# One decoder step on one core: the last gate's product on plain f32 operands, with the third tile's column halves side by side

## The chip, the cores and the metric

One core of a Trainium2 chip runs the whole step as one program. The metric is the device time in microseconds; lower is better. The engines are TensorE (PE, with its weight loads shown as PEld), VectorE (DVE), ScalarE (ACT), GpSimd (POOL) and SyncE (SP, which here only issues DMAs). They run their own instruction streams and meet at semaphores.

## The reference, cut to what matters

The step takes 256 prompt tokens and 64 sample tokens (8 sequences of 8), 320 rows of 1024 columns, through one layer. All that matters for the change is its last part:

```python
x1 = layer_norm(ALPHA * x + merged @ w_o, ln1_g, ln1_b)
x2 = layer_norm(ALPHA * x1 + hier_moe(x1), ln2_g, ln2_b)
gate = sigmoid(x2 @ w_ple_gate + b_ple_gate)      # (320, 1024) @ (1024, 1024)
pe = p_emb @ w_ple                                # (320, 256) @ (256, 1024)
x3 = layer_norm(ALPHA * x2 + gate * pe, ln3_g, ln3_b)
```

All inputs and outputs are f32.

## The kernel before, in words

The 320 rows lie in three tiles of 128, 128 and 64 rows (`TILES`, `ROWS`). Weights pass through `ring`, 12 slots of 128 x 2048 f32 (8 KB in each partition); SP fills a slot when the last reader of its former content has signalled. The program goes: input projection and attention, mixing and first norm, routing, 32 experts, and the tail. Everything up to the last expert is the same in both kernels.

**Precision.** PE takes two kinds of operands here. Plain f32 operands give one matmul that the trace shows as two records. Rounded operands (float32r, made by `rounded`) give one record. Before the change the gate's product is put together from rounded parts: an operand is cast to a high part, the low part is what the cast left out, and three products are summed (high x high, low x high, high x low). `by_parts` (L1387) writes this for the output projection w_o (L1625) and for the gate (L1856).

**The tail, in the order of its steps.**

1. The expert results lie transposed and sorted in `YsT`. `turn_sorted` (L1819) turns them back by PE, ten halves of 512 columns through banks 6 and 7; ACT casts each half to `yj_high` (L804), DVE subtracts to `yj_low` (L1311), and `combine` (L1828, matmuls at L1833) sums them into banks 0 to 5, one for each tile's column half. The first tile's combining is interleaved with the turns; the other two tiles follow in 40 matmuls. A turn may only begin when DVE's subtraction has freed its bank (`yt_v`).
2. Between these steps ACT and DVE prepare the gate's weights from the four ring slots of `w_ple_gate` (slots 1 to 4): ACT casts eight pieces of 128 x 1024 to `gw_high` (`high_gate`, L796 to L800) and DVE makes eight pieces of `gw_low` (`low_gate`, L1291 to L1295), each written into its engine's program at a fixed place.
3. DVE adds the residual (`combined`, L1285) and runs the second norm (`norm2`, L1305): statistics, their combination, one pass, a wait for ACT's square root (`norm`, L699), a reciprocal and a last pass. `layer_norm` (L1058) is the shared body.
4. `turn_tile` (L1376, transposes at L1384) turns a tile of x2 on PE, ACT casts the columns to `x2_high` (`high_columns`, L810) and DVE makes the low columns (`low_columns`, L1297).
5. PE runs six gate jobs (L1847 to L1857), two column halves of 512 for each tile, in turn into banks 7 and 6. For tiles 0 and 1 a job is 24 matmuls of 128 x 128 by 512 columns. For tile 2 the 64 high and 64 low rows lie side by side in one stationary operand of 128 columns (`x2_high` is 64 columns longer for this); a job is 8 such matmuls and 8 of the low weights, and its result stands in two halves of the bank's partitions, to be added. The turn of tile 1 stands before job 1, that of tile 2 before job 3. Job j waits for the bias add of job j - 2 (`pg_add`).
6. For each job DVE adds the bias (`gates`, L1329; for tile 2 a second add, L1337, brings in the other half of the partitions), ACT takes the sigmoid (`gate_out`, L816), POOL multiplies by the embedding (L543), and DVE adds the residual (`residual`, L1340). Then `norm3` (L1348) and SP's store of the tile (L458).

The order on DVE at the end is written out by hand (L1351 to L1365): gates(0), low_columns(1), norm2(2), gates(1), residual(0), norm3(0), gates(2), low_columns(2), gates(3), residual(1), gates(4), norm3(1), gates(5), residual(2), norm3(2). ACT's order (L823 to L837) is as fixed. An engine that waits holds up all that stands behind it in its own stream.

One product in the kernel already runs on plain f32 operands with the third tile's halves side by side: the embedding product p @ w_ple (L1783 to L1792), five jobs of two steps of the inner dimension, which runs once between the experts.

Of the kernel before, what the change touches and what calls it, by code (L numbers as in the profile page):

```python
# [10 lines left out]
ALU = mybir.AluOpType  # L11
# [103 lines left out]
def hybrid_step(nc, a):  # L115

    ctx = ExitStack()
    with ctx:
# [115 lines left out]
        x2_high = rounded("x2_high", 73728, [P, KD, T + ROWS[2]])  # L234
        x2_low = rounded("x2_low", 86016, [P, KD, PROMPT])

        gw_high = rounded_in_ring("gw_high", 8, [P, 4, KD, 256])
        gw_low = rounded_in_ring("gw_low", U_GATE % RING, [P, 4, KD, 256])
# [6 lines left out]
        def tiny(*shape):  # L245
# [75 lines left out]
        x2t_ps, x2t_v, x2t_a, pg_ps, pg_add, pg_sig, pg_mul = map(  # L321
            sem, ("x2t_ps", "x2t_v", "x2t_a", "pg_ps", "pg_add", "pg_sig", "pg_mul"))
# [224 lines left out]
        def _(act):  # L547
# [248 lines left out]
            def high_gate(n):  # L796

                c, k = n // 2, slice(4 * (n % 2), 4 * (n % 2) + 4)
                act.wait_ge(w_in_slot[slot_of(U_GATE + c)], 16 * turn_of(U_GATE + c))
                nc.scalar.copy(gw_high[:, c, k], unit(slot_of(U_GATE + c), KD)[:, k]).then_inc(wh_set, 1)  # L800

            for g in range(10):
                act.wait_ge(yt_ps, g + 1)
                nc.scalar.copy(yj_high[:, g // 2, half_of(g)], bank[6 + g % 2][:, :]).then_inc(yt_a, 1)  # L804
                if g % 2 == 1:
                    high_gate(g // 2)
            for n in range(5, 8):
                high_gate(n)

            def high_columns(t):  # L810

                for g in range(2):
                    act.wait_ge(x2t_ps, 2 * t + g + 1)
                    nc.scalar.copy(x2_high[:, 4 * g:4 * g + 4, P * t:P * t + ROWS[t]], four(bank[2 * t + g], ROWS[t])).then_inc(x2t_a, 1)
# [9 lines left out]
            high_columns(0)  # L824
            norm(5)
            high_columns(1)
            gate_out(0)
            norm(6)
            gate_out(1)
            norm(7)  # L830
            high_columns(2)
# [9 lines left out]
        def _(dve):  # L841
# [449 lines left out]
            def low_gate(n):  # L1291

                c, k = n // 2, slice(4 * (n % 2), 4 * (n % 2) + 4)
                dve.wait_ge(wh_set, Z_JOBS + 2 * KD + 4 + n + 1)
                V.tensor_tensor(gw_low[:, c, k], unit(slot_of(U_GATE + c), KD)[:, k], gw_high[:, c, k].bitcast(F32), ALU.subtract).then_inc(wl_set, 1)  # L1295

            def low_columns(t):  # L1297

                for g in range(2):
                    dve.wait_ge(x2t_a, 2 * t + g + 1)  # L1300
                    c = slice(4 * g, 4 * g + 4)
# [587 lines left out]
```

## Time and profile before

| | us |
|---|---|
| runs: median (lowest to highest) | 614.47 (611.05 to 615.39), 3 runs |
| the profiled execution, its own time | 612.5 |
| its span, first to last instruction | 610.8 |
| the tail, from the first turn of expert results (537.3) on | 73.5 of the span |

The profile is of one execution. Times in its rows are microseconds from the start of the span. Its views are: the page (busy time of each engine), the chain of waits (the work that ended last, followed back from the end, here read in order of time), timelines of one engine or all, weight loads of PE apart from its matmuls, groups of instructions by line and shape, and stretches of time with the busy time of each engine and TensorE's granted clock (1.00 is 2.4 GHz). In a row, `L1406` is a line of the kernel, `out<-in` the tensors, `x8` the number of records merged into it, and the bracket the idle time of the engine ahead of it with what ended it. A matmul's record is longer than the distance to the next one's start, since matmuls overlap.

### The profile page before, as it was taken

To read this page: it belongs to the slowest core of one execution; us is meant where nothing else is said; L and a number is where in the kernel's file an instruction comes from. 1 tells how busy PE (TensorE), PEld (TensorE's weight loads), DVE (VectorE), ACT (ScalarE), POOL (GpSimd) and SP (SyncE) were. 2 spreads that over 40 slices of the span, in tenths; PEclk is the share of its full clock that TensorE was granted. 3 is DMA by queue.
4 is the path that set the end of the run, shared out by engine and by line. 5 is a ranking of instruction groups with operands and counts; after the bars stand their busy time and mean duration, and the time that the engine had idled before them with its cause. 6 is when DMAs were issued, how large, how long until landed. Compare 5 with 4: busy or idle time off the path is not lost.

```text
span 610.8 us, 9501 instructions
## 1 busy us (share of the span) xinstructions
PE 535.9 (88%) x3628; PEld 390.4 (64%) x3628; DVE 287.9 (47%) x614; ACT 193.0 (32%) x363; POOL 57.6 (9%) x86
## 2 busy tenths in 40 slices
PE   3999879999999979869997979797979798978990
PEld 2999778888999967658554545353535444455770
DVE  2443786654683876796221212121222212278976
ACT  3444444442553250324311111111111121164432
POOL 2100003321625300000000000000000000000121
PEclk9999989999999999759998989898989999979996
DMA  9995336755225900691499999999999998900001
GB/s 278 367 312 177 121 113 204 248 187 194 100 70 170 300 33 0 253 418 54 158 419 409 412 414 418 413 418 417 418 416 420 414 418 314 372 6 0 2 34 52
DMA packets 51643, 151.86 MB, mean 249 GB/s; under 512 B 3088, under 2 KB 27861, under 8 KB 43280
## 3 DMA queue, kind: packets, MB, share of 16 engines
q1 hardware_dynamic: 47058, 137.72, 59.2%
q0 software_dynamic: 3728, 12.08, 6.2%
q10 hardware_dynamic: 822, 1.59, 0.8%
q8 instruction: 23, 0.38, 0.3%
q14 instruction: 12, 0.10, 0.0%
HBM read 148.59 MB, written 2.90 MB: 248 GB/s over the span
## 4 chain that ended last, share of the span: by engine, by line
PE 72%; DVE 12%; DVEq 5%; issue 4%; ACT 3%; DMA 2%; POOL 0%; POOLq 0%; SPq 0%
PE bank L1722 18%; PE bank L1427 16%; PE bank L1406 8%; PE bank L1735 8%; DVEq L1232 5%; PE bank L1614 5%; PE bank L1744 3%; PE bank L1833 2%; PE bank L1384 2%; PE bank L1790 1%; PE bank L1728 1%; DMA arena<-in_cache_k_dram 1%; DMA arena<-in_x_sample_dram 1%; PE bank L1481 1%; DVE arena L1224 1%
## 5 line engine op out<-in xcount | busy, mean ns | idle before, releaser
L1722 PE MATMUL bank<-ring,arena 128*64 128x256 f32 x1024 | 129.0, 396 | 0.9 <-DVE arena L1212 0.9
L1722 PEld LDWEIGHTS bank<-ring,arena 128*64 128x64 f32 x1024 | 72.9, 141 | 52.6 <-issue 21.6
L1224 DVE TENSOR_TENSOR arena<-bank,arena 128x512 f32 x32 | 22.1, 692 | 150.0 <-PE bank L1744 150.0
L1427 PE MATMUL bank<-x_high,w_high 128*128 128x320 f32 x256 | 83.4, 326 | 2.7 <-DVE w_low L871 2.7
L1427 PE MATMUL bank<-x_low,w_high 128*128 128x320 f32 x256 | 80.7, 315 | 0.0
L1427 PE MATMUL bank<-x_high,w_low 128*128 128x320 f32 x256 | 80.6, 315 | 0.0
L1735 PE MATMUL bank<-ring,arena 128*64 128x512 f32 x256 | 62.5, 609 | 0.0
L871 DVE TENSOR_TENSOR w_low<-ring,w_high 128x1024 fp32r<-128x1024 f32 x32 | 40.1, 1259 | 32.0 <-ACT w_high L564 31.9
L1427 PEld LDWEIGHTS bank<-x_high,w_high 128*128 128x128 f32 x256 | 49.7, 194 | 4.2 <-issue 4.1
L1427 PEld LDWEIGHTS bank<-x_low,w_high 128*128 128x128 f32 x256 | 49.8, 195 | 0.1
L1427 PEld LDWEIGHTS bank<-x_high,w_low 128*128 128x128 f32 x256 | 49.5, 193 | 0.0
L752 ACT COPY arena<-bank 128x512 f32<-128x512 f32 x32 | 18.8, 586 | 70.8 <-PE bank L1735 70.8
L543 POOL TENSOR_TENSOR arena<-arena 128x512 f32<-128x512 f32 (+1 forms) x6 | 7.7, 1286 | 328.3 <-ACT arena L821 328.3
L564 ACT CAST w_high<-ring 128x1024 fp32r<-128x1024 f32 x32 | 33.0, 1040 | 0.2 <-DMA ring<-in_w_in_dram 0.2
L1735 PEld LDWEIGHTS bank<-ring,arena 128*64 128x64 f32 x256 | 15.7, 137 | 24.2 <-issue 24.1
L1728 PE MATMUL bank<-cst,arena 128*128 128x128 f32 x32 | 10.7, 334 | 21.9 <-DVE arena L1219 21.9
L748 ACT COPY arena<-bank 128x128 f32<-128x128 f32 x32 | 8.5, 266 | 65.3 <-PE bank L1728 65.3
L1217 DVE TENSOR_TENSOR arena<-bank,arena 128x128 f32<-128x128 f32 x32 | 9.3, 291 | 41.8 <-issue 36.2
L743 ACT ACTIVATE arena<-bank 128x128 f32<-128x128 f32 x32 | 8.9, 278 | 59.2 <-PE bank L1722 59.2
L1728 PEld LDWEIGHTS bank<-cst,arena 128*128 128x128 f32 x32 | 4.5, 139 | 35.1 <-DVE arena L1219 25.8
L1744 PEld LDWEIGHTS bank<-cst,arena 128*128 128x128 f32 x128 | 14.1, 146 | 15.1 <-issue 12.9
L1744 PE MATMUL bank<-cst,arena 128*128 128x128 f32 x128 | 22.0, 297 | 1.1 <-ACT arena L752 1.1
(295 smaller groups left out, 883.0 us busy)
## 6 DMA issues: line engine op xcount, KB each, us to landing
ring<-in_w_gate_dram SPq DMA_DIRECT2D x32, 1024.0 KB, 10.3
ring<-in_w_up_dram SPq DMA_DIRECT2D x32, 1024.0 KB, 11.4
ring<-in_w_down_dram SPq DMA_DIRECT2D x32, 1024.0 KB, 8.6
ring<-in_w_in_dram SPq DMA_DIRECT2D x16, 1024.0 KB, 9.2
arena<-in_cache_k_dram POOLq DMA_DIRECT2D x16, 256.0 KB, 3.9
arena<-in_cache_v_dram POOLq DMA_DIRECT2D x16, 256.0 KB, 3.4
ring<-in_w_o_dram SPq DMA_DIRECT2D x4, 1024.0 KB, 10.4
ring<-in_w_ple_gate_dram SPq DMA_DIRECT2D x4, 1024.0 KB, 10.6
```

What stands on the lines that cost most here:

```text
L564: nc.scalar.copy(w_high[:, j % 4], unit(slot_of(j // 2), KD)[:, :, P * (j % 2):P * (j % 2 + 1)]).then_inc(wh_set, 1)
L752: nc.scalar.copy(y_s[:], bank[3][:, :]).then_inc(q["ys"], 1)
L871: V.tensor_tensor(w_low[:, j % 4], unit(slot_of(j // 2), KD)[:, :, P * (j % 2):P * (j % 2 + 1)], w_high[:, j % 4].bitcast(F32), ALU.subtra ...
L1224: V.tensor_tensor(YsT[:, :, bass.ds(place, WIN)].rearrange("p (d c) n -> p c d n", d=2), b[:, :].rearrange("p (c d n) -> p c d n", c=4, d= ...
L1232: return dve.value_load(start_i[0:1, 0, bass.ds(e, 1)], min_val=0, max_val=PAIRS)
L1406: last = mm(b[0:x.shape[1], 256 * q0:256 * q1].rearrange("p (s n) -> p s n", n=256), x, w[:, 2 * hf + q0:2 * hf + q1, k, :], start=(n == 0 ...
L1427: last = mm(bank[j % 2][:, 0:T], w[:, j % 4, k, :], x[:, k, :], start=(k == n == 0), stop=(k == KD - 1 and n == 2))
L1614: last = mm(bank[2 * w + n % 2][:, 0:T], wp[:, j % 4, 4 * w + k, :], yp_[:, k, :], start=(k == m == 0), stop=(k == 3 and m == 2))
L1722: last = mm(b[WIN * f:WIN * (f + 1), 0:256].rearrange("p (s n) -> p s n", s=2), x[:, WIN * k:WIN * (k + 1)], w[:, :, k, P * f:P * (f + 1)] ...
L1728: nc.tensor.transpose(bank[2][:, 0:P], hh[:], ident).then_inc(q["ht"], 1)
L1735: last = mm(bank[3][WIN * d:WIN * (d + 1), :], hT[:, WIN * f:WIN * (f + 1)], unit(slot, 2)[:, f, 512 * d:512 * (d + 1)], start=(f == 0), s ...
L1744: last = nc.tensor.transpose(b[:, P * c:P * (c + 1)], y_s[:, P * c:P * (c + 1)], ident)
```

## The change

The rounded copies `x2_high`, `x2_low`, `gw_high` and `gw_low` go, with the ACT casts and DVE subtractions that made them. ACT copies the turned columns of x2 plainly into `x2T` (f32). PE multiplies `x2T` with the ring slots of `w_ple_gate` directly: plain f32, eight matmuls of 512 columns for each job of tiles 0 and 1. Tile 2 has one job (j = 4) in place of two: for each of the eight inner steps it issues two matmuls of 64 stationary columns, the left half's result to partitions 0 to 63 and the right half's to partitions 64 to 127 of bank 7 (`tile_position`). The bias adds of tile 2 are one add for each half, and both wait for that job. On DVE, norm2(2) stands ahead of gates(0); on ACT, norm(6), its square root, stands ahead of the copies of tile 1 and of gate_out(0). PE itself waits for the four ring slots.

```diff
@@ -231,11 +231,8 @@
             (RING_AT, RING_AT + 4 * D, RING_AT + 4 * (UNIT * 7 + D), ARENA + 22528, ARENA + 88064))]
         x2 = at(61440, [P, TILES, D])
 
-        x2_high = rounded("x2_high", 73728, [P, KD, T + ROWS[2]])
-        x2_low = rounded("x2_low", 86016, [P, KD, PROMPT])
-
-        gw_high = rounded_in_ring("gw_high", 8, [P, 4, KD, 256])
-        gw_low = rounded_in_ring("gw_low", U_GATE % RING, [P, 4, KD, 256])
+        x2T = at(73728, [P, KD, T])
+
         gt = at(38912, [P, TILES, D])
         ln2, ln3, bpg = ring[:, 5, :], ring[:, 6, :], ring[:, 7, 0:D]
 
@@ -318,8 +315,8 @@
         over = {n: sem("over_" + n) for n in steps + ("w", "freed")}
         moe_done = sem("moe_done")
         yt_ps, yt_v, yt_a, cm_ps, cm_used = map(sem, ("yt_ps", "yt_v", "yt_a", "cm_ps", "cm_used"))
-        x2t_ps, x2t_v, x2t_a, pg_ps, pg_add, pg_sig, pg_mul = map(
-            sem, ("x2t_ps", "x2t_v", "x2t_a", "pg_ps", "pg_add", "pg_sig", "pg_mul"))
+        x2t_ps, x2t_a, pg_ps, pg_add, pg_sig, pg_mul = map(
+            sem, ("x2t_ps", "x2t_a", "pg_ps", "pg_add", "pg_sig", "pg_mul"))
         late_here, y_set, x2_set = map(sem, ("late_here", "y_set", "x2_set"))
         stored = sem("stored")
         chain_v = sem("chain_v")
@@ -793,25 +790,15 @@
                     hidden_out(over, n + 1)
                     result_out(over, n + 1)
 
-            def high_gate(n):
-
-                c, k = n // 2, slice(4 * (n % 2), 4 * (n % 2) + 4)
-                act.wait_ge(w_in_slot[slot_of(U_GATE + c)], 16 * turn_of(U_GATE + c))
-                nc.scalar.copy(gw_high[:, c, k], unit(slot_of(U_GATE + c), KD)[:, k]).then_inc(wh_set, 1)
-
             for g in range(10):
                 act.wait_ge(yt_ps, g + 1)
                 nc.scalar.copy(yj_high[:, g // 2, half_of(g)], bank[6 + g % 2][:, :]).then_inc(yt_a, 1)
-                if g % 2 == 1:
-                    high_gate(g // 2)
-            for n in range(5, 8):
-                high_gate(n)
-
-            def high_columns(t):
+
+            def turned_columns(t):
 
                 for g in range(2):
                     act.wait_ge(x2t_ps, 2 * t + g + 1)
-                    nc.scalar.copy(x2_high[:, 4 * g:4 * g + 4, P * t:P * t + ROWS[t]], four(bank[2 * t + g], ROWS[t])).then_inc(x2t_a, 1)
+                    nc.scalar.copy(x2T[:, 4 * g:4 * g + 4, P * t:P * t + ROWS[t]], four(bank[2 * t + g], ROWS[t])).then_inc(x2t_a, 1)
 
             def gate_out(n):
 
@@ -821,14 +808,14 @@
                 nc.scalar.activation(v, v, ACT.Sigmoid).then_inc(pg_sig, 1)
 
             norm(4)
-            high_columns(0)
+            turned_columns(0)
             norm(5)
-            high_columns(1)
+            norm(6)
+            turned_columns(1)
             gate_out(0)
-            norm(6)
             gate_out(1)
             norm(7)
-            high_columns(2)
+            turned_columns(2)
             gate_out(2)
             gate_out(3)
             gate_out(4)
@@ -1288,20 +1275,6 @@
                 t, c = j // 2, half_of(j)
                 V.scalar_tensor_tensor(x2[0:ROWS[t], t, c], x1[0:ROWS[t], t, c], ALPHA, bank[j][0:ROWS[t], :], ALU.mult, ALU.add).then_inc(cm_used, 1)
 
-            def low_gate(n):
-
-                c, k = n // 2, slice(4 * (n % 2), 4 * (n % 2) + 4)
-                dve.wait_ge(wh_set, Z_JOBS + 2 * KD + 4 + n + 1)
-                V.tensor_tensor(gw_low[:, c, k], unit(slot_of(U_GATE + c), KD)[:, k], gw_high[:, c, k].bitcast(F32), ALU.subtract).then_inc(wl_set, 1)
-
-            def low_columns(t):
-
-                for g in range(2):
-                    dve.wait_ge(x2t_a, 2 * t + g + 1)
-                    c = slice(4 * g, 4 * g + 4)
-                    dst = x2_low[:, c, P * t:P * (t + 1)] if t < 2 else x2_high[:, c, T:T + ROWS[2]]
-                    V.tensor_tensor(dst, four(bank[2 * t + g], ROWS[t]), x2_high[:, c, P * t:P * t + ROWS[t]].bitcast(F32), ALU.subtract).then_inc(x2t_v, 1)
-
             def norm2(t):
                 dve.wait_ge(cm_used, 2 * t + 2)
                 layer_norm(x2, t, ln2[:, 0:D], ln2[:, D:2 * D], TILES + t + 1, x2_set)
@@ -1309,33 +1282,22 @@
             for g in range(10):
                 dve.wait_ge(yt_a, g + 1)
                 V.tensor_tensor(yj_low[g // 2][:, half_of(g)], bank[6 + g % 2][:, :], yj_high[:, g // 2, half_of(g)].bitcast(F32), ALU.subtract).then_inc(yt_v, 1)
-                if g % 2 == 1 and g < 9:
-                    low_gate(g // 2)
             dve.wait_ge(late_here, 80)
             combined(0)
             combined(1)
             norm2(0)
-            for n in range(4, 6):
-                low_gate(n)
             combined(2)
             combined(3)
-            low_columns(0)
-            for n in range(6, 8):
-                low_gate(n)
             norm2(1)
             combined(4)
             combined(5)
 
             def gates(j):
 
-                dve.wait_ge(pg_ps, j + 1)
-                t, c, b = j // 2, slice(512 * (j % 2), 512 * (j % 2 + 1)), bank[7 - j % 2]
-                v = gt[0:ROWS[t], t, c]
-                last = V.tensor_tensor(v, b[0:ROWS[t], :], bpg[0:ROWS[t], c], ALU.add)
-                if t == 2:
-                    link(last)
-                    last = V.tensor_tensor(v, v, b[64:P, :], ALU.add)
-                last.then_inc(pg_add, 1)
+                dve.wait_ge(pg_ps, min(j, 4) + 1)
+                t, c = j // 2, slice(512 * (j % 2), 512 * (j % 2 + 1))
+                z = bank[7 - j % 2][:, :] if t < 2 else bank[7][64 * (j % 2):64 * (j % 2) + 64, :]
+                V.tensor_tensor(gt[0:ROWS[t], t, c], z, bpg[0:ROWS[t], c], ALU.add).then_inc(pg_add, 1)
 
             def residual(t):
 
@@ -1348,14 +1310,12 @@
             def norm3(t):
                 layer_norm(x2, t, ln3[:, 0:D], ln3[:, D:2 * D], 2 * TILES + t + 1, y_set)
 
+            norm2(2)
             gates(0)
-            low_columns(1)
-            norm2(2)
             gates(1)
             residual(0)
             norm3(0)
             gates(2)
-            low_columns(2)
             gates(3)
             residual(1)
             gates(4)
@@ -1844,17 +1804,24 @@
                     combine(n, t)
             turn_tile(x2, 0, x2t_ps, x2_set)
 
-            for j in range(6):
+            first = U_GATE % RING
+            for c in range(4):
+                weights(U_GATE + c)
+            for j in range(5):
                 t = j // 2
                 if j in (1, 3):
                     turn_tile(x2, (j + 1) // 2, x2t_ps, x2_set)
                 pe.wait_ge(x2t_a, 2 * t + 2)
-                pe.wait_ge(x2t_v, 2 * t + 2)
 
                 if j >= 2:
                     pe.wait_ge(pg_add, j - 1)
-                by_parts(bank[7 - j % 2], j, lambda k, c0, c1: x2_high[:, k, c0:c1], lambda k, c0, c1: x2_low[:, k, c0:c1],
-                         gw_high, gw_low, 4).then_inc(pg_ps, 1)
+                for k in range(KD):
+                    for hf in ((j % 2,) if t < 2 else (0, 1)):
+                        p0 = 64 * hf if t == 2 else 0
+                        w = ring[:, first + 2 * hf:first + 2 * hf + 2, :].rearrange("p s (k n) -> p s k n", k=KD)[:, :, k, :]
+                        last = mm(bank[7 - j % 2][p0:p0 + ROWS[t], :].rearrange("p (s n) -> p s n", n=256),
+                                  x2T[:, k, P * t:P * t + ROWS[t]], w, start=(k == 0), stop=(k == KD - 1), tile_position=(0, p0))
+                last.then_inc(pg_ps, 1)
 
 
 # ---- launch: one core; inputs and outputs as the reference has them ----
```

## Rows read from the trace of the kernel before

**Rows 1.** The page: the span, and the engines' busy time

```profile
span 610.8 us, 9501 instructions
...
PE 535.9 (88%) x3628; PEld 390.4 (64%) x3628; DVE 287.9 (47%) x614; ACT 193.0 (32%) x363; POOL 57.6 (9%) x86
```

**Rows 2.** The chain of waits from 536 us on: start us, us, what

```profile
544.00 1.07 ACT yj_high L804 x2
545.08 0.96 ACT gw_high L800
...
546.06 1.23 DVE gw_low L1295
...
548.48 1.13 DVE gw_low L1295
...
550.87 10.40 PE bank L1833 x44
...
562.36 1.29 DVE x_low L1303 x2
563.64 2.27 DVE gw_low L1295 x2
...
583.23 9.50 PE bank L1406 x40
...
592.82 0.69 DVE arena L1334
...
593.54 0.70 DVE arena L1337
```

**Rows 3.** Timeline of PE, 536 to 611 us: start, length, operation [idle before]

```profile
537.30 1.94 PE L1825 MATMUL bank<-cst,arena 128*128 128x128 f32 x8 [2.56 <-issue]
...
563.75 0.47 PE L1406 MATMUL bank<-gw_high,x_high 128*128 128x512 f32 x1 [1.61 <-ACT x_high L814]
...
570.31 1.09 PE L1384 MATMUL bank<-cst,arena 128*128 128x128 f32 x8 [0.74 <-DVE arena L1070]
571.15 0.47 PE L1406 MATMUL bank<-gw_high,x_high 128*128 128x512 f32 x1
...
582.52 0.70 PE L1384 MATMUL bank<-cst,arena 64*128 64x64 f32 x8
583.16 0.50 PE L1406 MATMUL bank<-gw_high,x_high 128*128 128x512 f32 x1
```

**Rows 4.** Timeline of all engines, 590 to 611 us

```profile
598.89 0.68 DVE L1334 TENSOR_TENSOR arena<-bank,ring 64x512 f32<-64x512 f32 x1
...
607.46 0.52 SPq L458 DMA_DIRECT2D out_y_sample_dram<-arena  x1
```

**Rows 5.** Timeline of PE, 492 to 505 us

```profile
492.11 1.94 PE L1735 MATMUL bank<-ring,arena 128*64 128x512 f32 x8
493.98 9.00 PE L1790 MATMUL bank<-ring,arena 128*128 128x512 f32 x24
502.81 1.90 PE L1722 MATMUL bank<-ring,arena 128*64 128x256 f32 x16
```

**Rows 6.** Timeline of PE's weight loads, 492 to 505 us

```profile
494.51 0.19 PEld L1790 LDWEIGHTS bank<-ring,arena 128*128 128x128 f32 x1 [0.24 <-issue]
494.94 0.19 PEld L1790 LDWEIGHTS bank<-ring,arena 128*128 128x128 f32 x1 [0.24 <-issue]
```

**Rows 7.** PE's groups by line and shape, whole run: busy us, mean ns | idle before

```profile
L1790 PE MATMUL bank<-ring,arena 128*64 128x512 f32 x8 | 1.9, 605 | 0.0
```

**Rows 8.** Groups by line and shape, 536 to 611 us: busy us, mean ns | idle before

```profile
L1295 DVE TENSOR_TENSOR gw_low<-ring,gw_high 128x1024 fp32r<-128x1024 f32 x8 | 9.6, 1220 | 0.5 <-ACT gw_high L800 0.3
...
L1311 DVE TENSOR_TENSOR yj_low<-bank,yj_high 128x512 fp32r<-128x512 f32 x10 | 6.5, 685 | 3.3 <-ACT yj_high L804 3.2
```

**Rows 9.** Stretches of 8 us: PE, PEld, DVE, ACT, POOL busy, granted clock, DMA

```profile
536.00:544.00 8.00, 6.15 (x26) 5.10 (x27) 4.45 (x6) 4.24 (x6) 0.00 (x0) 0.57 0.01 4
...
560.00:568.00 8.00, 6.39 (x32) 4.92 (x31) 6.50 (x11) 1.28 (x3) 0.00 (x0) 1.00 0.01 2
```

## The prediction

> **What bounds the kernel now.** I read the page first, then the chain of waits over the last 75 us, then the timelines of the engines in it. The page [rows 1] shows TensorE (PE) busy for 88% of the span, VectorE (DVE) for under half. The change touches only what follows the experts, so the tail has to be read by itself, and there the chain [rows 2] changes engine several times:
>
> - Up to 550.87 PE waits for the copies and subtractions that split the expert results. Among them, on the same engines, stand casts that prepare the gate's weights: one high part on ScalarE (ACT) at 545.08, two low parts on DVE at 546.06 and 548.48.
> - From 550.87 it is PE alone for 10.40 us: 44 combining products, unbroken.
> - Then x2's first tile is turned and split (its low columns at 562.36), and the gate's jobs begin at 563.75 [rows 3]. After job 0 PE sat idle 0.74 us before the turn at 570.31, for the second tile's norm, which stood on DVE behind two more low parts (563.64).
> - From 571.15 PE sets the pace to 583.23 + 9.50 = 592.73 [rows 2], the end of the fifth job. The end belongs to DVE: adding the bias in two adds (592.82, 593.54), a whole norm of tile 1 queued in between, the same two adds for the last half [rows 4], then sigmoid, gate times embedding, residual and last norm; the last store is issued at 607.46.
>
> So PE's products set the tail, with about 2.5 us lost to casts.
>
> **The change, part by part.**
>
> *The products.* Before, a job of tiles 0 and 1 is 24 matmuls of 512 columns on rounded operands. Jobs 1 and 2 together take 571.15 to 582.52 with the gap before the turn [rows 3], 48 matmuls: 11.37/48, or 0.235 us each, 5.6 us for a job. After, a job is 8 matmuls on plain f32. The trace has exactly this operation: the embedding product, 128 x 128 stationary by 512 columns f32. Each of its matmuls is two records, and the weight loads of successive records start 0.43 us apart (494.51, 494.94) [rows 5, 6]. So a matmul is 0.86 us, a job 8 x 0.86 = 6.88 us: 1.3 us longer, four times.
>
> *The third tile.* Before, two jobs of 16 matmuls, 16 x 0.235 = 3.7 us each. After, one job of 8 pairs, left and right half at once, on 64 columns of the array each. The embedding product does this too: its 24 records are 16 full ones and 8 of 64 columns [rows 7], and from 493.98 to the next line's start at 502.81 are 8.83 us [rows 5]; 16 x 0.43 leaves 1.95 us for two pairs, which is 4 steps of 0.43 and 0.2 for the change of width. So a pair costs what one full matmul costs: 6.88 + 0.2 for the whole tile. PE as a whole gets dearer only by the four jobs, but now *both* halves come at the end of a 7 us job, where before the first came 3.7 us ahead of the second.
>
> *Casts gone, ahead of the gate.* The eight low parts (9.6 us on DVE) [rows 8] and eight high parts go. What is late next: the subtraction of expert results itself. From 544.00, when the fifth and sixth half are copied, a round is a turn by PE (0.45), a copy (two in 1.07), a subtraction (0.69), two halves interleaved, with 4 combining matmuls, 0.94 us, between rounds [rows 2, 8]. Walking it: subtractions end 545.9 (as before, the earlier casts filled idle time); turns of the next two halves 545.4 to 546.4; their subtractions end 547.2 and 547.85; the last turns 547.3 to 548.4; the last subtraction ends 549.85. Combining starts at 549.9 instead of 550.87: 1.0 us gained of the 3.3 us of casts on the chain there.
>
> *Columns of x2.* The turned tile is copied plainly, at the same cost as the rounded copy. The low columns vanish. The first of two subtractions started 562.36 when the first copy was done; the second copy is done some 0.55 later, so job 0 starts near 562.9 instead of 563.75: 0.85 us. Together job 0 starts at 561.9.
>
> *The norms.* A norm takes DVE 593.54 + 0.70 to 598.89, 4.65 us [rows 2, 4]; its variance is there after some 1.8. With 1.4 us for the two residual adds ahead of each, and job 0's combining 1.0 earlier, norm of tile 0 ends near 556.5 and norm of tile 1 follows at 557.9. Its square root on ACT stands behind the copies of tile 0 (done near 561.9), so it ends near 563.6, long before job 0 does (568.8): the 0.74 us idle goes. Norm of tile 2 is moved ahead of the first bias add; it runs 565.0 to 569.6, and the add that it delays is wanted only by job 2 at 576.6, 6 us later. On ACT its square root stands ahead of tile 1's copies; its variance is there at 566.8, before those copies are due (569.3). If that cover of 2.5 us went, each late us would be a us on PE. On SP and POOL nothing is passed: POOL's product and the stores wait for the same semaphores as before.
>
> *The sum on PE.* Starts: job 0 561.9; + 6.88, 0.1 gap, 0.84 for the turn (570.31 to 571.15) gives job 1 at 569.7, job 2 at 576.6, end 583.5; turn of tile 2 0.1 + 0.64 (582.52 to 583.16) gives job 3 at 584.2, job 4 at 591.1 + 0.2. Its last record starts 15 x 0.43 later and takes 0.6 (24 records overlap to 9.00 where their starts span 8.4): PE ends at 598.35. The adds before began 0.09 after PE's end (592.73 to 592.82), so now at 598.4 instead of 592.82: 5.6 us later.
>
> *Behind it.* The order on DVE stays: add of the first half, norm of tile 1, add of the second half, and so on. All of tile 1's norm (about 594.2 to 598.9 before) again runs only after job 4 is awaited, though its input is ready some 3.5 us after job 3's end at 591.1 (add, sigmoid, product, residual). Two adds of the chain go (the second add of each half, 0.7 each with its link): 1.35 us. From the first add to the last store were 607.46 - 592.82 = 14.64; now 13.3: store issued at 611.7, 4.2 us later than before.
>
> The profiled execution took 612.5 us around its span of 610.8; by the sum the same execution becomes 616.7. The median of the runs is 614.5, 2 us above it; with the sum on that median the forecast is 618.7, and I take 618.5. That is 0.7% more, inside the 1% that a measurement of this kernel can tell from no change.
>
> **The rivals.**
>
> *A. The casts come back in full (not slower).* The chain shows 0.96 + 1.23 + 1.13 + 1.29 + 2.27 = 6.9 us of casts [rows 2]; my sum credits 1.85 at the start and 0.74 for the idle, 2.6. If all came back, 4.3 us more go, and the kernel stays at 614.4. This needs job 0 to start at or before 557.7. Against: the 44 products in 10.40 us have no cast between them, and the turn of tile 0 stands behind them on PE.
>
> *B. A step of f32 is longer than 0.43 us.* The expert's down products, 64 wide, go from 492.11 to 493.98 in 4 steps [rows 5]: 0.47. With 0.47 in all 80 steps the tail gains another 3.2 us: 621.9. For: gaps between bursts; against: the embedding product is the same shape, and its starts are 0.43 apart for 16 records.
>
> *C. The halves of tile 3 overlap only in part.* If they ran one after another, job 4 would be 6.9 us longer: 625.5. The trace's 1.95 us for two pairs speaks against it. The Trainium skill (TensorE: Matmul & The Clock Gate, section Measured speedup vs the span model) gives three tiles side by side a speedup of 2.38, not 3; an estimate by that ratio makes job 4 8.7 us and the time 620.3. This trace, with two tiles side by side, shows no such loss.
>
> *D. PE falls to its low clock.* From 536 to 544 the granted clock was 0.57, mostly the 1.2 GHz level, where 1.00 is 2.4 [rows 9]; PE had stood idle 2.56 us ahead of 537.30 [rows 3]. Such a stretch inside the gate costs half its length, 4 us: 622.7. Against: PE paused 1.61 us ahead of job 0 and the clock stayed at 1.00 [rows 3, 9], and the change leaves only 0.8 us ahead of job 0. The other way, a shorter low stretch at 536 gives up to 2.5 us back, with or without the change.
>
> **How the numbers follow.** My own sum 0.65; B 0.13; D 0.09; C 0.06; A 0.07. The sum's own range is 616 to 621 (the start of job 0 by 0.8 us, the gaps by 0.5, the runs' spread of 611 to 615.4). 614.5 takes in A, 622 takes in B; what lies beyond is most of C and D. Slower by over 1% is above 620.6: most of B, C and D and the upper edge of the sum, 0.25. Faster by over 1%, under 608.3, no case gives: 0.02. Within 1%: 0.73.
>
> **What would show it.** Right: records of the gate's line 0.43 us apart, 96 in all (64 full, 32 of 64 columns); job 0 near 562, job 4's end near 598; no idle of PE ahead of the second turn; DVE idle some 3 us ahead of job 4's end and then doing tile 1's norm; the chain's last part add, norm, add, sigmoid, product, residual, norm. Wrong: a start of job 0 before 558 (A); starts 0.47 apart (B); pairs in which the second starts after the first ends (C); granted clock below 1 after 562 (D). Were job 4's end near 598 but the end not 4 us later, the adds behind it would be mispriced.

## The result, and the profile after

The changed kernel takes 618.71 us (median of 20 runs, 615.67 to 623.24), the kernel before 613.99 us on the same chip (20 runs, 611.05 to 617.78). The ratio is 1.0072, with a 95% interval of 1.0051 to 1.0093: 0.7% slower, an effect that exists but lies inside 1%. The forecast was 618.5 us.

The tail can be cut at five points that both kernels have: the end of the experts (DVE's last small write there), the start of combining's unbroken stretch of 44 products, the start of job 0, PE's last product, the issue of the last store. "Forecast" is the prediction's own walk, in the times of the profiled execution before.

| stretch of the profiled execution, us | before | forecast | after |
|---|---|---|---|
| start of span to end of experts | 535.90 | as before | 538.43 |
| to the start of the 44 products | 14.97 | 14.0 | 15.78 |
| to the start of job 0 | 12.88 | 12.0 | 12.06 |
| to PE's last product | 32.64 | 36.4 | 36.43 |
| to the issue of the last store | 11.07 | 13.3 | 13.30 |
| from the 44 products to the last store | 56.59 | 61.8 | 61.79 |

Three terms came out as walked, the second did not, and the first is time in which both kernels run the same instructions.

The page of the changed kernel, which answers to [rows 1]: the span, and the engines' busy time.

```profile
span 619.3 us, 9410 instructions
...
PE 544.2 (88%) x3596; PEld 384.8 (62%) x3596; DVE 274.4 (44%) x598; ACT 182.8 (30%) x353; POOL 57.4 (9%) x86
```

DVE and ACT lost 13.5 and 10.2 us of work (287.9 - 274.4, 193.0 - 182.8), and PE gained 8.3. Of these 8.3, 4.5 lie between the start of job 0 and PE's last product (36.4 us busy against 31.9), and 3.0 ahead of PE's first turn, where both kernels run the same instructions. Where the time went in the tail is in the chain of waits of the changed kernel from 536 us on, which answers to [rows 2]: start us, us, what.

```profile
538.43 0.07 DVE misc L1270
538.50 1.94 issue
540.44 1.10 PE bank L1785 x4
...
552.87 1.30 DVE yj_low L1284 x2
...
554.21 10.37 PE bank L1793 x44
564.58 0.45 PE bank L1344 x4
...
565.05 1.08 ACT arena L801 x2
566.14 0.14 issue
566.27 7.10 PE bank L1822 x16
573.38 0.87 PE bank L1344 x8
574.25 13.73 PE bank L1822 x32
587.99 0.64 PE bank L1344 x8
588.62 14.11 PE bank L1822 x48
```

No cast of a weight is left in it. From 566.27 on the chain is PE alone for 36.5 us: job 0, a turn, jobs 1 and 2, a turn, jobs 3 and 4. PE's timeline shows that no gap stands before the second turn, where [rows 3] had 0.74 us (start, length, operation, idle before).

```profile
566.27 7.10 PE L1822 MATMUL bank<-ring,arena 128*128 128x512 f32 x16 [0.82 <-ACT arena L801]
573.21 1.04 PE L1344 MATMUL bank<-cst,arena 128*128 128x128 f32 x8
574.09 13.90 PE L1822 MATMUL bank<-ring,arena 128*128 128x512 f32 x32
```

The groups by line and shape, 538 to 604 us (busy us, mean ns | idle before), have the 96 records that were forecast, 64 full and 32 on 64 columns.

```profile
L1822 PE MATMUL bank<-ring,arena 128*128 128x512 f32 x64 | 28.1, 595 | 0.8 <-ACT arena L801 0.8
...
L1822 PE MATMUL bank<-ring,arena 128*64 128x512 f32 x32 | 7.1, 595 | 0.0
```

Behind PE's end the timeline of all engines, 598 to 620 us, answers to [rows 4].

```profile
602.82 0.68 DVE L1300 TENSOR_TENSOR arena<-bank,ring 64x512 f32<-64x512 f32 x1 [3.66 <-PE bank L1822]
603.43 1.27 DVE L1049 BATCH_NORM_STATS2 small<-arena 128x6 f32<-128x512 f32 x2
...
606.82 1.28 DVE L1057 SCALAR_TENSOR_TENSOR arena<-arena,small,ring 128x1024 f32<-128x1024 f32 x1
...
608.14 0.69 DVE L1300 TENSOR_TENSOR arena<-bank,ring 64x512 f32<-64x512 f32 x1
...
616.00 0.52 SPq L455 DMA_DIRECT2D out_y_sample_dram<-arena  x1
```

DVE sat idle 3.66 us ahead of the first bias add, while tile 1's norm stood ready behind that add in its queue; then the norm (603.43 to 608.10) held up the second add, whose sum had been in PSUM since PE's end.

### The profile page after: what moved, and what is told of

Its sections match the earlier page's. It is cut to its first block, busy times and chain, and to the rows that moved or that the text cites. A ratio compares the mean times of both kernels' runs of the same rounds, so it can differ in the third digit from the quotient of the medians.

```text
span 619.3 us, 9410 instructions
## 1 busy us (share of the span) xinstructions
PE 544.2 (88%) x3596; PEld 384.8 (62%) x3596; DVE 274.4 (44%) x598; ACT 182.8 (30%) x353; POOL 57.4 (9%) x86
## 4 chain that ended last, share of the span: by engine, by line
PE 76%; DVE 10%; DVEq 5%; issue 4%; ACT 2%; DMA 2%; POOL 0%; POOLq 0%; SPq 0%
PE bank L1682 18%; PE bank L1387 16%; PE bank L1695 8%; PE bank L1822 6%; PE bank L1366 5%; DVEq L1219 5%; PE bank L1574 5%; PE bank L1704 3%; PE bank L1793 2%; PE bank L1344 1%; PE bank L1750 1%; PE bank L1688 1%; PE bank L1441 1%; PE bank L1785 1%; DMA arena<-in_x_sample_dram 1%
## 5 line engine op out<-in xcount | busy, mean ns | idle before, releaser
L1822 PE MATMUL bank<-ring,arena 128*128 128x512 f32 (+1 forms) x96 | 35.2, 595 | 0.8 <-ACT arena L801 0.8
L1688 PE MATMUL bank<-cst,arena 128*128 128x128 f32 x32 | 10.5, 328 | 21.9 <-DVE arena L1206 21.9
L1822 PEld LDWEIGHTS bank<-ring,arena 128*128 128x128 f32 (+1 forms) x96 | 14.1, 172 | 19.7 <-issue 19.7
L1688 PEld LDWEIGHTS bank<-cst,arena 128*128 128x128 f32 x32 | 4.4, 138 | 35.2 <-DVE arena L1206 25.9
## 6 DMA issues: line engine op xcount, KB each, us to landing
ring<-in_w_up_dram SPq DMA_DIRECT2D x32, 1024.0 KB, 12.3
```

Source lines behind the costliest of these rows:

```text
L1688: nc.tensor.transpose(bank[2][:, 0:P], hh[:], ident).then_inc(q["ht"], 1)
L1822: last = mm(bank[7 - j % 2][p0:p0 + ROWS[t], :].rearrange("p (s n) -> p s n", n=256), x2T[:, k, P * t:P * t + ROWS[t]], w, start=(k == 0), ...
```

## The experiments

All changes are against the changed kernel unless the kernel before is named. Ratios are to the kernel before, with 95% intervals.

**1. The norm ahead of the add it stands behind.** The waits on DVE and ACT keep their meaning; only the order of two queues changes.

```
-            gates(4)
             norm3(1)
+            gates(4)
             gates(5)
...
-            gate_out(4)
             norm(8)
+            gate_out(4)
             gate_out(5)
```

> The changed kernel, with tile 1's last norm ahead of the first bias add of tile 2 on DVE (its square root ahead of that half's sigmoid on ACT). My theory: after PE's end DVE does a norm that could have run before it; moved, it falls into DVE's 3.7 us of idle time, and what is left behind PE's end is add, add, sigmoid, product, residual, norm. About 4.6 us go: from PE's last product to the last store 8.6 us instead of 13.2, and the time is that of the kernel before within 0.3% (ratio near 1.000). Rival: the product on POOL or the last job itself holds the end, and the order is worth under 1 us (ratio 1.006 or more).

Measured: 1.0025 (1.0001 to 1.0049), median 615.61 us. By the ratios 0.47% came back, 2.9 us; in the trace the stretch from the 44 products to the last store is 58.85 us instead of 61.79, also 2.9. So the direction is right and the size is not: 4.6 was expected. DVE's timeline of this kernel, 595 to 613 us, shows both halves of the shortfall.

```profile
596.65 1.29 DVE L1049 BATCH_NORM_STATS2 small<-arena 128x6 f32<-128x512 f32 x2
...
599.79 1.28 DVE L1057 SCALAR_TENSOR_TENSOR arena<-arena,small,ring 128x1024 f32<-128x1024 f32 x1
601.00 1.40 DVE L1300 TENSOR_TENSOR arena<-bank,ring 64x512 f32<-64x512 f32 x2
603.71 2.33 DVE L1307 SCALAR_TENSOR_TENSOR arena<-arena 64x512 f32<-64x512 f32 x2 [1.31 <-POOL arena L540]
606.07 1.28 DVE L1049 BATCH_NORM_STATS2 small<-arena 64x6 f32<-64x512 f32 x2
```

The idle time was 3.7 us and the norm takes 4.4 here, so it ran over: PE ended at 600.16, 0.09 later it would have let the adds go, and they began at 601.00, 0.75 us late. And with both adds at once, POOL's two products of gate and embedding ran one behind the other, so that from the first add to the store 9.49 us passed; with the norm's 4.65 taken from the changed kernel's 13.18 it would have been 8.53. 4.65 - 0.75 - 0.96 = 2.94. The norm between the adds had been hiding the first half's sigmoid and product; moved away, it uncovered them.

**2. The same order in the kernel before.** Is this something that the change brought, or was it lying there? The edit is the same one.

> The kernel before, with the same order as the run norm first (tile 1's last norm ahead of tile 2's bias adds). My theory: there tile 1's residual ends 592.5 and the fifth job 592.7, so the norm has no idle time to fall into; it delays both adds of the fifth job by what it takes and saves the same behind them: the last norm begins within 1 us of where it did, ratio to the kernel before 0.998 to 1.001. So what the order gave on the changed kernel (2.9 us) is the price of waiting for both halves in one job. Rival: the order is better whatever the products are; then the same 2.9 us here (0.995).

Measured: 0.9994 (0.9963 to 1.0025), and 56.39 us instead of 56.59 from the 44 products to the store, in one profile of each. In the kernel before the first half's sum is there 3.7 us ahead of the second's, and DVE is hardly idle ahead of its first add (DVE's timeline of the kernel before, 590 to 599 us):

```profile
592.82 0.68 DVE L1334 TENSOR_TENSOR arena<-bank,ring 64x512 f32<-64x512 f32 x1 [0.32 <-PE bank L1406]
```

So the norm has 0.32 us of idle time to fall into, not 3.66; moved, it delays both adds by about what it takes and saves about the same behind them. The old order costs 0.2 us there, and 2.9 with both halves at PE's end. That much of the change's loss is an order on DVE that it made unfit; the theory that the order was bad anyway falls.

**3. The third tile's halves one after another.** The second half's result then goes to bank 6, and its add reads it there.

```
-            for j in range(5):
+            for j in range(6):
...
-                    for hf in ((j % 2,) if t < 2 else (0, 1)):
+                    for hf in (j % 2,):
...
-                dve.wait_ge(pg_ps, min(j, 4) + 1)
+                dve.wait_ge(pg_ps, j + 1)
```

> The changed kernel, with the third tile's column halves as two jobs, one after the other, still plain f32. My theory: halves side by side run at the price of one, so apart they cost 6.9 us more on PE, in 16 steps of 0.43 each; but tile 1's norm stands between the two adds and hides 5.3 us of the second job, so the end comes only 1.6 us later than in the changed kernel (ratio to the kernel before near 1.010). Rival 1: halves side by side do not overlap; then PE's time does not change and the end is the same (1.007). Rival 2: PE sets the end one to one; then 6.9 us later (1.018).

Measured: 1.0067 (1.0041 to 1.0092), and 61.81 us from the 44 products to the store against 61.79. PE works 5.2 us longer (41.64 from job 0 to its end, not 36.43) and the end does not move: a loss of 1.6 was expected, none came. DVE's timeline of this kernel, 599 to 607 us:

```profile
600.25 0.68 DVE L1300 TENSOR_TENSOR arena<-bank,ring 64x512 f32<-64x512 f32 x1 [3.66 <-PE bank L1822]
...
604.25 1.29 DVE L1057 SCALAR_TENSOR_TENSOR arena<-arena,small,ring 128x1024 f32<-128x1024 f32 x1
605.56 0.69 DVE L1300 TENSOR_TENSOR arena<-bank,ring 64x512 f32<-64x512 f32 x1
```

The second add waits for the norm, which ends at 605.54; PE's last product ended at 605.35. The whole second half is computed under cover of the norm. Side by side, then, buys nothing in this order of the queue; with test 1's order, where the second add waits for PE, it should, but that pair was not tried. And PE got 5.2 us longer, not the 6.9 of a job. The weight loads of PE, 592 to 601 us, say why (the view does not name the half that a load belongs to).

```profile
597.83 0.14 PEld L1822 LDWEIGHTS bank<-ring,arena 128*64 128x64 f32 x1 [0.29 <-issue]
598.26 0.19 PEld L1822 LDWEIGHTS bank<-ring,arena 128*64 128x64 f32 x3 [0.29 <-issue]
598.69 0.19 PEld L1822 LDWEIGHTS bank<-ring,arena 128*64 128x64 f32 x2 [0.24 <-issue]
599.12 0.19 PEld L1822 LDWEIGHTS bank<-ring,arena 128*64 128x64 f32 x2 [0.23 <-issue]
599.61 0.14 PEld L1822 LDWEIGHTS bank<-ring,arena 128*64 128x64 f32 x1 [0.29 <-issue]
```

One load every 0.43 us is one half alone. From 598.26 to 599.12 there are several, four more than one half needs: by these loads the second half's first four steps run on the other 64 columns of the array beside the first half's last ones, and 4 x 0.43 is the 1.7 us that are missing (6.9 - 5.2).

**4. PE's products taken away in part.** This kernel leaves out two of the eight steps of each job of tiles 0 and 1, and with them a quarter of each of their sums.

```
+                steps_ = KD - 2 if t < 2 else KD
-                for k in range(KD):
+                for k in range(steps_):
```

> The changed kernel, with two of the eight inner steps left out in the jobs of tiles 0 and 1 (their gates are sums over 768 of the 1024 columns). That takes 2 x 0.86 us off each of four jobs, 6.9 us of PE. My theory: PE sets the pace from job 0 to its end without a gap, so the whole 6.9 us come off, and the ratio to the kernel before is near 0.996. Rival: DVE and ACT between the jobs (norms, adds) hold PE back when it is faster; then PE shows idle time behind the second turn and 3 us or less come off (1.002 or more).

Measured: 0.9962 (0.9934 to 0.9991), median 611.68 us. From the 44 products to the store 54.92 us, 6.87 less than the changed kernel: 4 x 2 x 0.86 = 6.88. The chain of waits of this kernel from 554 us on has each job shorter by what was taken.

```profile
566.62 5.39 PE bank L1823 x12
572.01 0.88 PE bank L1344 x8
572.88 10.30 PE bank L1823 x24
```

So each us of product in these jobs is a us of the kernel, and nothing else holds PE back when each job is 1.7 us shorter. It also says what the change cost there: 1.3 us a job, four times.

**5. The casts kept.** The eight high and eight low parts are made as before, at their old places, into memory that nothing reads.

```
+                if g % 2 == 1:
+                    high_gate(g // 2)
...
+                if g % 2 == 1 and g < 9:
+                    low_gate(g // 2)
...
+            for n in range(4, 6):
+                low_gate(n)
...
+            for n in range(6, 8):
+                low_gate(n)
```

> The changed kernel, with the eight casts on ACT and eight subtractions on DVE for the gate's weights kept where they stood, into memory that nobody reads. My theory: they cost 1.0 us ahead of the combining (the last subtraction of expert results late) and nothing behind it, since the second tile's norm is wanted only when job 0 ends: the ratio to the kernel before near 1.009, and PE idle ahead of the combining of the last pair as before (some 1 us more than without them). Rival: the casts on the chain before were worth their 6.9 us in full; then 4 us or more (1.014).

Measured: 1.0113 (1.0067 to 1.0159) in four runs, median 620.12 us. From the 44 products to the store 61.78 us, as without the casts: of the half of them that stood behind, none costs anything now. The timelines of DVE and PE of this kernel, 563 to 572 us, say why.

```profile
566.95 1.29 DVE L1068 SCALAR_TENSOR_TENSOR arena<-arena,small,ring 128x1024 f32<-128x1024 f32 x1
570.55 1.04 PE L1367 MATMUL bank<-cst,arena 128*128 128x128 f32 x8
```

With the casts ahead of it, tile 1's norm ends at 568.24, 2.3 us before job 0 lets the second turn begin. The job's extra 1.3 us is only a part of that lead, and by this the casts would be free with the old job length as well. Most of the rest is the low columns, which are gone in this kernel too: in the kernel before DVE waited 1.43 us for the first copy of them and worked 1.29 us on them, ahead of that norm. By these numbers the idle time of 0.74 us in [rows 3] would have gone with the low columns alone. For the casts ahead of the 44 products the run is inconclusive: the median is 1.4 us above the changed kernel's, the interval is almost 6 us wide, and in its profile the 44 products began *earlier* after the experts than in any other, 12.96 us. In that execution PE started its first turn 0.11 us after the experts, where the changed kernel's profile has 2.01.

**6. The clock ahead of the combining held up, in both kernels.** The experts' last turns are followed by six products of 256 columns whose result is read by nobody.

```
             turn_result(main, EXPERTS, bank[5])
+            for _w in range(6):
+                mm(bank[0][:, 0:256], ones[:, :], cst[:, 0:256], start=True, stop=True)
```

> The changed kernel, with six plain f32 products of 256 columns (2.6 us, their result is overwritten unread) on PE behind the last expert's last transposes, where PE is idle. My theory: the low clock at the tail's start follows from this idle stretch, and which way it falls differs from run to run; with PE busy the granted clock stays near 1.00 there, the first two turns and the first combining run at full speed, and the combining's unbroken stretch begins some 12.5 to 13 us after the experts' end instead of 13.6 to 15.9: 1 to 3 us less than the changed kernel (ratio to the kernel before 1.003 to 1.005). Rival: PE is given the low clock by the sparse work of the turns themselves; then the clock falls all the same and the time is that of the changed kernel (1.007).

> The kernel before, with the same six products in PE's idle stretch. My theory: the clock stays up, and the unbroken combining begins 13 to 13.5 us after the experts' end instead of 15.0 (casts on DVE then set the pace): 1.5 to 2 us less, ratio 0.997. Rival as in the run warm: no change (1.000), or worse where the six products hold up the first turn.

The reason to do this is in the stretches of 4 us (PE, PEld, DVE, ACT, POOL busy, granted clock, DMA). First the kernel before:

```profile
534.00:538.00 4.00, 1.36 (x8) 1.15 (x9) 0.75 (x2) 0.03 (x1) 0.00 (x0) 0.83 0.15 55
538.00:542.00 4.00, 3.45 (x16) 2.77 (x15) 2.54 (x4) 2.91 (x5) 0.00 (x0) 0.50 0.01 4
542.00:546.00 4.00, 3.97 (x21) 2.87 (x19) 3.78 (x6) 3.32 (x5) 0.00 (x0) 0.82 0.00 0
```

Then the changed kernel:

```profile
538.00:542.00 4.00, 1.56 (x8) 1.57 (x8) 0.21 (x2) 0.43 (x1) 0.00 (x0) 0.60 0.02 4
542.00:546.00 4.00, 3.45 (x13) 2.57 (x12) 2.35 (x4) 1.91 (x4) 0.00 (x0) 0.50 0.01 4
546.00:550.00 4.00, 4.00 (x19) 3.42 (x19) 1.80 (x3) 1.17 (x2) 0.00 (x0) 0.62 0.00 0
```

Both fall to the 1.2 GHz level (0.50) after PE's idle time at the experts' end; the changed kernel stayed near it for some 3 us more in its profile (0.62 in the third stretch, where the kernel before has 0.82). That hides what the casts were worth. With the fillers the granted clock is 1.00 from 538 to 546 us in both kernels. The rows that matter in PE's timelines are the first turn and the first of the 44 products; the kernel before with fillers:

```profile
540.53 1.06 PE L1827 MATMUL bank<-cst,arena 128*128 128x128 f32 x8 [1.68 <-issue]
...
552.80 0.50 PE L1835 MATMUL bank<-yj_high,Pj 128*128 128x512 f32 x1 [0.75 <-DVE yj_low L1311]
```

The changed kernel with fillers:

```profile
541.28 1.06 PE L1787 MATMUL bank<-cst,arena 128*128 128x128 f32 x8 [1.52 <-issue]
...
552.15 0.50 PE L1795 MATMUL bank<-yj_high,Pj 128*128 128x512 f32 x1 [0.47 <-DVE yj_low L1284]
```

12.27 us with the casts, 10.87 without: at one clock they are worth 1.4 us by this pair of profiles, where the walk said 1.0. Without fillers the two profiles have 13.57 and 13.77. But with fillers the first turn starts later, 1.5 to 1.7 us after the last filler, in time that the profile calls "issue": 3.11 us after the experts' end in the kernel before (1.40 without fillers), 2.95 in the changed one (2.01). In the kernel before this takes back all of the 1.3 us that the clock gave, in the changed kernel 0.9 of 2.9. The ratios are 0.9983 (0.9955 to 1.0011) for the kernel before and 1.005 (1.002 to 1.0081) for the changed one; neither is clear of that without fillers.

**7. Half of the last product on DVE.** To test 1's order, the last half's gate times embedding goes to DVE, beside POOL's, and the residual takes that half first.

```
+                for hf in range(2 if t < 2 else 1):
...
+                    if t == 2 and hf == 1:
...
+                        link(V.tensor_tensor(g5, g5, pe_s[0:ROWS[t], t, 512:1024], ALU.mult))
```

> The run norm first, with the last half's gate times embedding on DVE instead of POOL. In norm first the two products of tile 2 run one behind the other on POOL (2.48 us from 602.41) while DVE is idle from 602.4 to 603.7. My theory: with one of them on DVE (0.7 us) the last norm begins 0.9 us earlier than in norm first, 5.0 us instead of 5.85 us after the fifth job's last product; ratio to the kernel before near 1.001. Rival: DVE and POOL slow each other on the same memory (DVE's passes took 1.54 instead of 1.27 us beside a product on POOL), and nothing is won (1.0025).

Measured: 1.0023 (0.9998 to 1.0048), 58.33 us from the 44 products to the store against test 1's 58.85: 0.5 us less, not 0.9. The timeline of all engines, 604.9 to 608 us:

```profile
605.11 1.25 POOL L540 TENSOR_TENSOR arena<-arena 64x512 f32<-64x512 f32 x1 [6.52 <-ACT arena L808]
...
605.78 1.12 DVE L1309 TENSOR_TENSOR arena<-arena 64x512 f32<-64x512 f32 x1 [0.69 <-ACT arena L808]
606.94 1.29 DVE L1313 SCALAR_TENSOR_TENSOR arena<-arena 64x512 f32<-64x512 f32 x2
```

The two residuals behind it, of the same shape, from SBUF like it and with POOL done, take 1.29 together, 0.65 each; DVE's product, 0.58 us of which lie beside POOL's (to 606.36), took 1.12.

**8. Everything together, on both kernels.** Order, half on DVE, and two fillers instead of six.

> The changed kernel with three edits: tile 1's last norm first, the last half's product on DVE, and two (not six) idle-filling products on PE, 0.86 us, so that they end about when the experts' end is signalled. My theory: the clock stays up and the first turn comes about 1.1 us after the experts' end, so the unbroken combining begins near 12 us after it, and the last store is issued 58.3 us behind that (as in the run half on DVE): 70.3 us, against 71.6 in the kernel before's profile and 70.7 in the run of the kernel before with the norm first. Ratio to the kernel before 0.997 to 1.000. Rival: 0.86 us do not fill the idle stretch, the clock falls, the combining begins 13.6 us or more after the experts' end: 1.002.

> The kernel before with the same three edits. My theory: with the clock up, the casts' pace puts the combining's start 12.3 us behind the first turn, 13.4 us after the experts' end; behind it 56.4 - 0.5 = 55.9 us to the last store: 69.3 us, some 2 us less than the kernel before: ratio 0.996 to 0.998, faster than both kernels. Rival: the clock falls all the same, 14.5 + 55.9: ratio 0.999 or above.

Measured: 1.0034 (1.0006 to 1.0062) for the changed kernel, 0.9998 (0.9974 to 1.0023) for the kernel before. Both miss. Two fillers didn't hold the clock, and PE paused a second time, in the middle of the first two turns (after 6 of their 8 records), in "issue"; PE's timeline of the changed kernel so edited:

```profile
536.84 0.85 PE L1793 MATMUL bank<-cst,arena 128*128 128x128 f32 x6 [1.63 <-issue]
539.66 1.54 PE L1793 MATMUL bank<-cst,arena 128*128 128x128 f32 x6 [1.98 <-issue]
```

Behind the 44 products the gains are there (58.34 us for the changed kernel, 55.98 for the kernel before, 0.6 under its own 56.59), but no kernel that does the whole work beat the kernel before by more than its interval.

## Why the prediction was right

**The products.** Right, by the operation that the trace of before already had. A job was to be 6.88 us: job 0 took 6.94 (566.27 to 573.21), the whole from job 0 to PE's end 36.43 against 36.4. Test 4 confirms the price of a matmul, 0.86, and that it is paid one to one. Rival B (0.47 a step) falls.

**The third tile.** Right: its 8 pairs, from their first record at 595.62 to PE's end at 602.70, took 7.08 us, where 15 x 0.43 and a last record of 0.6 make 7.05; jobs 3 and 4 together took 14.15 against 13.90 for jobs 1 and 2, and the 0.25 between them is the change of width, put at 0.2. Rival C falls; its price was too high besides, since two halves apart cost 5.2 us more and not 6.9 (test 3). The Trainium skill's speedup of 2.38 for three tiles side by side (TensorE: Matmul & The Clock Gate, section Measured speedup vs the span model) doesn't carry over to two halves of 64 columns: the estimate by it was 8.7 us for this job, which took 7.08.

**Columns of x2, and the idle time of 0.74.** Right: 12.06 us from the 44 products to job 0 where 12.0 was walked, and no wait ahead of the second turn. The norm of tile 2, moved ahead, ended at 573.4, 0.2 us after job 0, and the add behind it is wanted only by job 2, at 581.

**Behind PE's end.** Right: 13.18 us from the first add to the store against 13.3. That tile 1's norm would run only after job 4 is awaited, though its input was ready, is what the trace shows, and test 1 gives its price, 2.9 us.

**The casts ahead of the combining.** This is the mis-sized term, "Combining starts at 549.9 instead of 550.87: 1.0 us gained". In the profile the stretch from the experts' end got 0.8 us longer. The mechanism holds, as test 6 shows (1.4 us at one clock), but in this profile PE's first turn came 0.6 later and the low clock lasted longer, and these took more than it gave. The 0.8 itself says little: tests 1, 3, 4 and 7 run the same instructions there, and their profiles have 13.59, 13.99, 15.92 and 15.68 us beside this one's 15.78. That the low stretch could vary stood in the prediction, but only as a gain, "up to 2.5 us back".

**The sum.** From the 44 products to the last store +5.2 us was walked (4.2 net, with the 1.0 taken back out) and +5.20 measured. The profiled span differs by 8.5 us; 0.8 more is the lead-in (from the experts' end to the 44 products), and 2.5 lies ahead of the experts' end. That last part holds nothing that the change touches, and it varies from profile to profile: the experts' end was at 535.9 to 537.4 us in the four profiles with the old products and at 535.5 to 538.7 in the eight with the new. By the medians the change costs 4.7 us where 4.2 was forecast, on a base 0.5 below the 614.5 that the forecast started from; the two cancel, so the closeness of 618.5 to 618.71 is partly luck. Nor is the 4.7 accounted for to the end: 5.2 less the 1.4 of test 6 would be 3.8, and where the other 0.9 lies, in the lead-in or ahead of the experts' end, the runs do not separate. Rival A (all casts back) falls with the 44 products as unbroken as before; rival D is shown absent inside the gate: the granted clock was 1.00 from 560 to 600 us.

What sets the start of PE's first turn, 0.1 to 3.1 us after the experts' end over the kernels here, the traces show in part. Their DMA records have an instruction queue (queue 8, 23 packets of 16 KB in a run of either kernel). In eleven of the twelve profiles the first turn starts 1.5 to 1.9 us after one of its packets has landed (landed at 535.77, turn at 537.30 in the kernel before; 538.82 and 540.44 in the changed one). In the twelfth, the casts kept, that packet had landed by 533.93, and PE started 0.11 us after the experts' end. The second pause of test 8 ends 1.3 us after such a landing in the changed kernel and 1.5 in the kernel before. A branch of PE's program, `pe.If(crowded > 0)`, stands just ahead of the turns. So PE most likely waits there for its next instructions; this is read from times alone, and no run changed only that.

Two points stay open. The experts' end lies at 536.6 us in the mean of the four profiles with the old products and at 538.0 in that of the eight with the new. The difference is there by the first expert: DVE's first add of an expert's result starts at 304.7 to 309.2 us with the old products and at 306.6 to 310.4 with the new, and from there to the experts' end both groups take 228.2 to 231.6. The change touches nothing there, and twelve profiles are too few to tell the difference from chance. And how long the low clock lasts in an average execution is not known: the five profiles with the same instructions from the experts' end to the 44 products differ by 2.3 us there.

## What to carry to other kernels

Price a product that would be computed plainly by the same operation elsewhere in the trace, spacing of weight loads rather than length of a record, and check that nothing else on the path depended on how its results were staggered: here 2.9 of the 4.7 us lost came back when a norm was moved that had been nearly free between two results and stood in the way once they came together. Work taken off an engine that is not the bound is worth only what of it stood on the path: 13.5 us less on DVE bought some 4.4 there (1.4 ahead of the 44 products at one clock, 0.8 and 0.7 around job 0, 1.5 behind PE's end). And an order written by hand into a queue has to be worked out anew when the moment of a result moves, both for what now waits and for what the waiting had hidden.

## What the runs showed of the hardware

- *Two f32 jobs on different column halves overlap at the seam.* By the weight loads the second began on its 64 columns some 1.7 us before the first had finished on the other 64 (test 3), and two half-width jobs cost 12.3 us, not 13.8.
- *DVE's element-wise product takes longer beside POOL's.* One of 64x512 f32, both operands in SBUF, took 1.12 us, of which 0.58 lay beside POOL's product; residuals of that shape with POOL idle take 0.65 to 0.70 (test 7).
- *Fillers hold the clock and delay what follows.* Six filler products kept 1.00 through a stretch that otherwise falls to 0.50, and moved the first turn from 2.01 to 2.95 us after the experts' end in the changed kernel, from 1.40 to 3.11 in the kernel before; in both the gain in time lies within the intervals.
- *PE's start behind a branch follows the instruction queue.* In eleven of twelve profiles the first turn starts 1.5 to 1.9 us after a 16 KB packet of that queue has landed; that PE waits for it is inferred.
